# Early, one-by-one loads of the third expert weight set, and a Fourier channel transform on 258 columns

## The reference, cut to what matters

```python
def _fourier_mixer(h, w_out):
    hg = h.astype(jnp.float32).reshape(B, L, FOURIER_GROUPS, FOURIER_CG)   # 4 groups of 256 channels
    z = jnp.fft.fftn(hg, axes=(1, 3), norm='ortho').real.reshape(B, L, D_MODEL)
    return jnp.einsum('bld,de->ble', z.astype(h.dtype), w_out)

def _hier_moe(h, ...):
    ...                                  # router: softmax over 4 groups, top-2 of 4 experts in the best one
    hid = jax.nn.silu(jnp.einsum('td,edf->tef', t, w_gate)) * jnp.einsum('td,edf->tef', t, w_up)
    y = jnp.einsum('tef,te,efd->td', hid, gates.astype(hid.dtype), w_down)
```

## Time and profile before

| | |
|---|---|
| median of 3 runs | 1116.37 us (1115.34 to 1123.04) |
| profiled execution, its own time | 1114.05 us |
| span of that profile, first to last instruction | 1112.3 us |
| mean granted TensorE clock | 0.945 of 2.4 GHz |
| PE busy | 936.5 us, 84% of the span |
| ACT, DVE, POOL busy | 249.0, 224.4, 171.6 us |
| moved by DMA | 317.68 MB |

### The profile page before, as it was taken

One profiled execution on the slowest core, in us unless ns is written; L12 is line 12 of the kernel. 1 busy time (PEld: TensorE's weight loads), 2 busy tenths in 40 slices (PEclk: granted clock), 3 DMA queues, 4 the chain that ended last, 5 costly groups with the idle time before them and its releaser, 6 DMA issues.

```text
span 1112.3 us, 17281 instructions
## 1 busy us (share of the span) xinstructions
PE 936.5 (84%) x6715; PEld 517.7 (47%) x6716; DVE 224.4 (20%) x539; ACT 249.0 (22%) x451; POOL 171.6 (15%) x287
## 2 busy tenths in 40 slices
PE   2799999998999966998899995699949999887850
PEld 0355446654446453554455552364435555443420
DVE  1100355101544350000000101501330000000005
ACT  1111223221224031222222221420322222211112
POOL 2001002201001032121121120210212122111112
PEclk9899999998999977999999998799969999989995
DMA  9975464556442746999999965950436999999954
GB/s 380 315 285 224 153 228 153 199 227 229 151 149 95 309 171 262 418 423 419 420 417 425 418 264 205 411 233 18 178 109 254 418 375 418 418 425 422 419 221 167
DMA packets 68459, 317.68 MB, mean 286 GB/s; under 512 B 13252, under 2 KB 15588, under 8 KB 53184
## 3 DMA queue, kind: packets, MB, share of 16 engines
q1 hardware_dynamic: 54592, 290.68, 65.3%
q0 software_dynamic: 9856, 18.51, 4.7%
q10 hardware_dynamic: 3968, 7.87, 2.0%
HBM read 308.62 MB, written 17.38 MB: 293 GB/s over the span
## 4 chain that ended last, share of the span: by engine, by line
PE 39%; DMA 20%; DVE 5%; issue 2%; SPq 2%; ACT 1%; POOLq 0%; POOL 0%; DVEq 0%; ACTq 0%
PE ps L849 13%; DMA ring<-in_moe_w_down 10%; PE ps L856 9%; PE ps L745 7%; DMA deep<-in_moe_w_down 6%; DMA deep<-hrow,gi 2%; PE ps L766 2%; SPq L376 2%; PE ps L825 1%; PE ps L782 1%; PE ps L543 1%; DMA deep<-yrows 1%; DMA yrows<-deep,si 1%; DVE deep L1421 1%; PE ps L818 1%
## 5 line engine op out<-in xcount | busy, mean ns | idle before, releaser
L849 PE MATMUL ps<-ring,deep 128*64 128x256 f32 x1600 | 181.8, 384 | 14.4 <-DMA ring<-in_moe_w_up 10.4
L849 PEld LDWEIGHTS ps<-ring,deep 128*64 128x64 f32 x1600 | 118.9, 139 | 83.8 <-issue 14.8
L567 PE MATMUL ps<-deep,ring 128*128 128x384 f32 x384 | 129.2, 494 | 4.2 <-ACT deep L940 4.2
L1417 DVE TENSOR_TENSOR deep<-deep,ps 128x128 f32<-128x128 f32 x76 | 18.4, 284 | 439.3 <-PE ps L849 439.3
L856 PE MATMUL ps<-ring,deep 128*64 128x512 f32 x400 | 96.4, 626 | 8.3 <-DVE deep L1421 8.3
L567 PEld LDWEIGHTS ps<-deep,ring 128*128 128x128 f32 x384 | 72.7, 192 | 58.3 <-issue 10.1
L849 PE MATMUL ps<-deep 128*64 128x256 f32 x832 | 92.8, 379 | 3.9 <-DMA deep<-in_moe_w_up 3.4
L570 PE MATMUL ps<-ring,deep 128*128 128x512 f32 x192 | 87.9, 610 | 0.0
L745 PE MATMUL ps<-ring,deep 128*128 128x512 f32 x192 | 83.8, 594 | 1.4 <-ACT deep L1020 0.8
L849 PEld LDWEIGHTS ps<-deep 128*64 128x64 f32 x832 | 61.2, 137 | 39.0 <-issue 6.8
L501 PE MATMUL ps<-ring,scond 128*32 128x512 f32 x384 | 50.7, 649 | 21.8 <-DMA ring<-in_w_mod 21.0
(11 more groups left out here) (163 smaller groups left out, 809.2 us busy)
## 6 DMA issues: line engine op xcount, KB each, us to landing
ring<-in_w_mod SPq DMA_DIRECT2D x24, 2048.0 KB, 12.0
ring<-in_moe_w_gate SPq DMA_DIRECT2D x22, 2048.0 KB, 22.9
ring<-in_moe_w_up SPq DMA_DIRECT2D x22, 2048.0 KB, 27.7
ring<-in_moe_w_down SPq DMA_DIRECT2D x22, 2048.0 KB, 32.8
ring<-in_hgrn_w_in SPq DMA_DIRECT2D x10, 2048.0 KB, 8.6
deep<-in_moe_w_gate SPq DMA_DIRECT2D x10, 2048.0 KB, 20.6
deep<-in_moe_w_up SPq DMA_DIRECT2D x10, 2048.0 KB, 25.0
deep<-in_moe_w_down SPq DMA_DIRECT2D x10, 2048.0 KB, 30.7
```

The lines of the kernel that those rows point to most:

```text
L567: last = mm(bank[:, 0:T], W[:, k, b * P:(b + 1) * P], hT[:, k, :], start=(k == 0), stop=(k == KD - 1))
L849: last = mm(ps[g * SLOTS:(g + 1) * SLOTS, GU_BANK[j], 0:2 * P], xt[:, b, h * SLOTS:(h + 1) * SLOTS], slot3(S[j])[:, k, g * F // 2:(g + 1) ...
```

## The change

Two parts that don't depend on each other.

**Loads.** The third set's buffers are used in the order 8, 7, 6 (gate, up, down) rather than 6, 7, 8. SP no longer waits for `idx_ready` and `gathered`. Unit 6 (gate of expert 2, now buffer 8) waits for the sixth `n_tp` of the layer, that is, until PE has read all of `xn`; units 7 and 8 (buffers 7 and 6) wait for `hrow_out`.

**Fourier.** `dft_c` holds columns 0 to 128 of the cosines and of the sines: 258 columns. `U` shrinks in step. An output chunk of the lower 128 channels of a group reads columns 0 to 127 of both halves, one of the upper reads columns 1 to 128, with the sine matrix of the other sign (`dft_ctx` and `dft_lat` hold it as a third plane). The upper chunk comes out in reversed channel order, which the rows of the output weights, reversed in the same way ahead of the launch, make good. Number and shape of the later products (L778, L782, L745) stay.

```diff
--- before.py
+++ after.py
@@ -171,10 +171,11 @@
         mod_b += [spare[:, C512:2 * C512]] * 4
 
         fo = Area(work, TT * D)
-        U = fo.take(TT * 4 * C512).rearrange("p (t g n) -> p t g n", t=TT, g=4)
-        dft_c = fo.take(2 * C512).rearrange("p (k n) -> p k n", k=2)
-        dft_ctx = fo.take(2 * P).rearrange("p (c n) -> p c n", c=2)
-        dft_lat = fo.take(4 * 2 * P).rearrange("p (t c n) -> p t c n", t=2, c=2)
+        FOLD = P + 1
+        U = fo.take(TT * 4 * 2 * FOLD).rearrange("p (t g n) -> p t g n", t=TT, g=4)
+        dft_c = fo.take(2 * 2 * FOLD).rearrange("p (k n) -> p k n", k=2)
+        dft_ctx = fo.take(3 * P).rearrange("p (c n) -> p c n", c=3)
+        dft_lat = fo.take(2 * 3 * 2 * P).rearrange("p (t c n) -> p t c n", t=2, c=3)
         zT = work[:, 0:TT * D].rearrange("p (k t) -> p k t", k=KD)
         assert fo.n <= WORK - 2 * D
         mod_row.append(work[:, WORK - 2 * D:WORK - 2 * D + C512])
@@ -300,7 +301,7 @@
         MOD_AFTER = [2, 4, 6, 8, 10, 12, 14, 16, 22, 24, 26, 28, 30, 32, 34, 35]
         for phase, u in STREAM:
             place(phase, u, mod_slot(u) if phase == "mod" else u % 2)
-        MOE_SLOTS = [[3, 4, 5, 0, 1, 2, 6, 7, 8], [4, 5, 3, 0, 1, 2, 6, 7, 8]]
+        MOE_SLOTS = [[3, 4, 5, 0, 1, 2, 8, 7, 6], [4, 5, 3, 0, 1, 2, 8, 7, 6]]
         FIRST_UNITS = [0, 1, 2, 5, 3, 4, 6, 7, 8]
         moe_before = [list(uses)]
         for u in range(3 * NE):
@@ -377,9 +378,9 @@
 
                 for u in FIRST_UNITS:
                     if u == 6:
-                        sp.wait_ge(M[l]["idx_ready"], 1)
+                        sp.wait_ge(n_tp, 6 * NORM[f"m{l}"] + 6)
+                    elif u == 7:
                         sp.wait_ge(M[l]["hrow_out"], 16 * TT)
-                        sp.wait_ge(M[l]["gathered"], 16)
                     elif u < 6:
                         first_wait(u)
                     unit(u // 3, u // 3, u % 3)
@@ -763,7 +764,7 @@
                         if n >= 4:
                             pe.wait_ge(u_evac4, n - 3)
                         for k in range(2):
-                            last = mm(ps[:, 4 + n % 4, :], hT[:, 2 * g + k, t * P:(t + 1) * P], dft_c[:, k, :],
+                            last = mm(ps[:, 4 + n % 4, 0:2 * FOLD], hT[:, 2 * g + k, t * P:(t + 1) * P], dft_c[:, k, :],
                                       start=(k == 0), stop=(k == 1))
                         last.then_inc(u_done4, 1)
                 pe.wait_ge(u_evac4, 12)
@@ -772,14 +773,16 @@
                         pe.wait_ge(mod_evac, 6)
                     if k >= 4:
                         pe.wait_ge(z_evac, k - 3)
-                    g, o = k // 2, (k % 2) * P
+                    g, high = k // 2, k % 2
                     bank = ps[:, k % 4, :]
                     for c in range(2):
-                        mm(bank[:, 0:P], U[:, 0, g, c * 256 + o:c * 256 + o + P], dft_ctx[:, c, :],
+                        o = c * FOLD + high
+                        mm(bank[:, 0:P], U[:, 0, g, o:o + P], dft_ctx[:, c * (1 + high), :],
                            start=(c == 0), stop=(c == 1))
                     for t in range(2):
                         for c in range(2):
-                            last = mm(bank[:, P:T], U[:, 1 + t, g, c * 256 + o:c * 256 + o + P], dft_lat[:, t, c, :],
+                            o = c * FOLD + high
+                            last = mm(bank[:, P:T], U[:, 1 + t, g, o:o + P], dft_lat[:, t, c * (1 + high), :],
                                       start=(t + c == 0), stop=(t + c == 2))
                     last.then_inc(z_done, 1)
 
@@ -1126,7 +1129,7 @@
             modulate("a1", 1, 0)
             for n in range(12):
                 act.wait_ge(u_done4, n + 1)
-                A(U[:, n // 4, n % 4, :], ps[:, 4 + n % 4, :], ACT.Copy).then_inc(u_evac4, 1)
+                A(U[:, n // 4, n % 4, :], ps[:, 4 + n % 4, 0:2 * FOLD], ACT.Copy).then_inc(u_evac4, 1)
             for k in range(KD):
                 act.wait_ge(z_done, k + 1)
                 A(zT[:, k, :], ps[:, k % 4, 0:T], ACT.Copy).then_inc(z_evac, 1)
@@ -1695,10 +1698,10 @@
         return np.cos(a) / np.sqrt(m), np.sin(a) / np.sqrt(m)
 
     cc, sc = dft(256)
-    dft_c = np.concatenate([cc, sc], 1).reshape(2, P, 512).transpose(1, 0, 2)
+    dft_c = np.concatenate([cc[:, 0:P + 1], sc[:, 0:P + 1]], 1).reshape(2, P, 2 * P + 2).transpose(1, 0, 2)
     c1, s1 = dft(P)
-    dft_ctx = np.stack([c1, -s1], 1)
-    dft_lat = np.stack([cc, -sc], 1).reshape(2, P, 2, 256).transpose(1, 0, 2, 3)
+    dft_ctx = np.stack([c1, -s1, s1], 1)
+    dft_lat = np.stack([cc, -sc, sc], 1).reshape(2, P, 3, 256).transpose(1, 0, 2, 3)
     out = dict(const=const, masks=masks, pos=pos, dft_c=dft_c, dft_ctx=dft_ctx, dft_lat=dft_lat)
     return {k: np.ascontiguousarray(v, v.dtype if v.dtype == np.int32 else f) for k, v in out.items()}
 
@@ -1716,6 +1719,9 @@
 
     nc = _bacc.Bacc("TRN2", target_bir_lowering=False, num_devices=1)
     arrays = {n: _np.ascontiguousarray(inputs[n]) for n in _INS}
+    rows = arrays["fourier_w_out"].reshape(1, 4, 2, P, D)
+    arrays["fourier_w_out"] = _np.ascontiguousarray(
+        _np.stack([rows[:, :, 0], rows[:, :, 1, ::-1]], 2).reshape(1, D, D))
     arrays.update(shape_constants())
     io = {n: nc.dram_tensor(f"in_{n}", a.shape, _mybir.dt.from_np(a.dtype), kind="ExternalInput").ap()
           for n, a in arrays.items()}
```

## The result

The changed kernel takes 1111.24 us in the median of 7 runs (1108.91 to 1113.14), the kernel before 1118.96 (1115.34 to 1123.04): a ratio of 0.9929, 95% interval 0.9905 to 0.9953, or 7.9 us less. On the median that the forecast started from, 1116.37, that ratio gives 1108.4, inside the range and 3.6 above the forecast of 1104.8. The gain is two thirds of the 11.6 expected, and lies within 1% of no change.

A forecast was written before the change was run, and what follows sets the result against it. PE, busy nearly all the time, was taken to bound the kernel. Terms -10.2 - 0.2 - 2.7 + 1.5 = -11.6 us took the median from 1116.37 to 1104.8; range 1099 to 1112.

The forecast's parts named there:

- Forecast 10.4: Fourier stage, first half: 48 products at 0.218 rather than 0.43 us save 10.2, ACT's shorter last copy 0.2.
- The modulation weights: Fourier stage: weights land at 707.6 or a microsecond later, wanted at about 714.7 and 720, so they stay hidden.
- the rival built on it: Fourier stage: pitch ends midway between 0.216 and 0.43, saving 5.1; sum -6.5, 1109.9 us; chance 0.06.
- the one on the clock: Fourier stage: PE falls to the 1.2 GHz level, the 10.2 go, second half doubles; +16.8, 1133.2 us; chance 0.05.
- the 34 us of SP's waiting: SP's wait for each layer's first gather: removing it doesn't move later expert loads, which wait for freed buffers.
- the cost of the collision: First gathers meeting the tail of units 7 and 8: 0.5 us in layer 0, 1.0 in layer 1, 1.5 in all.
- the forecast's two loads: Units 7 and 8, after the hrow stores: landing near 423.5 in layer 0, 831.6 in layer 1.
- an overlap of a microsecond: Layer 1: the two loads land near 831.6, the first gather at 830.4; priced at 1.0 us.
- The chance of 0.14 for a collision: Rival: late stores make first gathers run inside units 7 and 8, costing 5.9 + 4.7 for 1.5; -2.5, 1113.9 us; chance 0.14.
- A term that was put at nothing: First expert pass of each layer: the forecast's sum holds no change for its products.
- second gathers' waits: PE's wait before the second transposes: the second gather no longer runs beside set three, gaining 2.28 + 0.46 = 2.7 us.
- the prediction's estimate by turns: DMA queues: a gather beside a load takes at most twice its time alone; full collision would cost 3.4 us per layer.

The follow-up runs named there:

- that part alone: Full change with the loads put back as before, keeping the 258 columns, timed against the kernel before: ratio 0.9902 (0.9873 to 0.9931).
- three experiments: 258 columns: units 7 and 8 held for the first gather, 0.9888; stores first, third load after second gather, 0.9896; the latter plus idle-time products, 0.9845.
- clean gathers in other kernels: 258 columns, against the kernel before: stores first, third load after second gather, 0.9896 (products 9.40, 9.27); all three loads after the second gather, 0.9915 (10.10).

## Why the prediction was partly right

**The Fourier part was right in size and place.** Forecast 10.4, in the trace 25.63 - 15.28 = 10.35, by the runs 0.0098 of 1119.54 = 11.0 for that part alone. The pitch of 258 columns follows from 16 matmuls in 3.73 us, 0.23 with their start; ACT's last copy took 0.39 for 258 columns. The modulation weights stayed hidden: no wait between the blocks. That a narrow product is paced by its weight load does not hold for these products, with 0.23 us at 258 columns against 0.43 at 512; the rival built on it falls. So does the one on the clock in the form it had (a whole stage at the lower level), though a small cousin of it showed in three experiments, 1.7 us.

**That the 34 us of SP's waiting are worth nothing was right**: 68.3 us of waits ahead of the third set became 43.8, the waits for `used` behind it grew by 27.9, and expert 3 is still issued at the end of expert 0 (444.82, as the second pass begins).

**The step that failed is the cost of the collision**, put at 0.5 and 1.0. Counted from each layer's output projection as above, the forecast's two loads land at 34.9 us and the gather, alone, at 35.1 in layer 0; in layer 1 at 35.1 and 33.9. In the trace the loads landed at 36.2 and 35.4 and the gathers at 36.5 and 36.0. So the gathers landed 1.4 and 2.1 later, 3.5 in place of 1.5. The reason differs by layer. In layer 0 the loads were late: unit 6 was to use only time that other transfers left free and the stores to end "some 2 us later", but they took 6.8 to 7.3 us rather than 2.6 and ended 4.2 later than they would have. Free time on the engines, summed, did not say in which order transfers land. In layer 1 the schedule held within 0.3, and the price was too low: by its own times the loads land 1.2 after the gather, which was called an overlap of a microsecond and priced at 1.0, but the gather landed 0.5 after the loads. In layer 0 the gather's own time grew by more, 2.27, since the routing issued it 0.9 sooner. The chance of 0.14 for a collision was too low, and its price there (5.9 and 4.7, the covered second gathers of before) too high: only the end of the loads was met.

**A term that was put at nothing**: the first pass's products took 1.26 and 0.75 us more, with more of them at the 1.2 GHz level. It is open whether the change did this. Products as long (9.40, 9.27, 10.10) stand behind clean gathers in other kernels, so it may be luck of this execution. Together: gathers +3.5, products +2.0, second gathers' waits -2.7, sum +2.8; the stretches give 0.3 + 2.3 = +2.6 in place of -1.2. With the Fourier part that is -7.7 in the trace, near the -7.9 (-10.6 to -5.3) of the runs. Of the 3.9 us that the trace falls short of the forecast, the gathers explain 2.0 and the products 2.0.

On the turns between queues, packet by packet, that the Trainium skill (DMA: Bandwidth & Descriptors, section Queues, rings and completion order) states: the first gathers beside loads, 5.66, 5.48 and 6.53 us, stay under twice the 3.4 alone, as the prediction's estimate by turns would have it; layer 0's stores, 7 against 2.6, and the second gather of before, 9.3, do not. The runs bear that estimate out as a bound for some transfers only.

## What to carry to other kernels

Before a load is moved earlier, ask which load behind it moves too: here the next one hung on a buffer that only a finished expert frees, so a 34 us wait was free. Then list the small transfers on the path that the moved load will meet, and price them by a row in which such a transfer ran beside a load and by when the load lands, not by the engines' free share. And look at the clock behind each wait: the first products took 8.5 to 10.1 us at a mixed clock and 7.1 in the layer where PE had been kept busy.

## What the hardware showed that was not expected

One 2 MB load, with two gate broadcasts of 512 KB beside it, made three 512 KB stores on another queue land after 7 us rather than 2.6, and the broadcasts, on a third queue, after 8.7 to 11.1 rather than 3.7 to 4.7; the last store was issued when that load was 0.2 us from landing. And work that nobody needs can pay: with 14 idle-time products a layer the granted clock through the routing was 1.00 and 0.88 rather than 0.68 and 0.75, and 5 to 6 us came off.
